# Expert slots of a mixture-of-experts stage: weight split first, output copy one slot later, gathers released by the transposes

## The reference, cut to what matters

```python
def hier_moe(h, w_group, b_group, w_expert, b_expert, w1, w3, w2):
    ...                                   # 4 groups x 8 experts, top 1 group, top 2 experts, weights
    hid = silu(einsum('td,edf->tef', t, w1)) * einsum('td,edf->tef', t, w3)   # d = 1024, f = 128
    hid = hid * combine[:, :, None]
    y = einsum('tef,efd->td', hid, w2)
```

## Time and profile before

| what | value |
|---|---|
| median of 3 runs | 2931.61 us (2927.03 to 2933.74) |
| profiled execution, its own time | 2928.18 us |
| its span | 2926.4 us |
| PE busy in the span | 2581.6 us (88%) |
| DVE, ACT, POOL busy | 1817.2, 921.5, 1474.8 us |
| slots of layer 0, first to last output copy | 374.1 to 598.6 us |
| slots of layer 1, first to last output copy | 1165.8 to 1393.5 us |

### The profile page before, as it was taken

The page is one execution under the profiler, slowest core; times in us unless marked ns, Lnnn a source line. Parts: engine busy times, 40 slices in busy tenths (PEclk is TensorE's granted clock), DMA queues, the critical chain, the costliest instruction groups (busy, mean ns, idle before and its releaser), DMA issues.

```text
span 2926.4 us, 36370 instructions
## 1 busy us (share of the span) xinstructions
PE 2581.6 (88%) x12686; PEld 2013.5 (69%) x12686; DVE 1817.2 (62%) x2136; ACT 921.5 (31%) x1315; POOL 1474.8 (50%) x1258
## 2 busy tenths in 40 slices
PE   4888799959999997999598999999964569999998
PEld 3765677747777776777386478888853558888887
DVE  6768765656777766656647376662259962666414
ACT  2023266723444423666212322221122221322102
POOL 4720333335444451333463047667767726776775
PEclk8978799979999997999698799999977889999999
DMA  8846478842323223887322023332420003333222
GB/s 302 265 139 220 158 273 299 294 129 81 94 94 100 86 87 109 310 291 259 127 75 70 1 56 88 100 100 90 123 75 1 1 1 87 94 93 100 94 94 79
DMA packets 316240, 375.70 MB, mean 128 GB/s; under 512 B 51258, under 2 KB 258894, under 8 KB 316022
## 3 DMA queue, kind: packets, MB, share of 16 engines
q1 hardware_dynamic: 258832, 326.14, 34.1%
q10 hardware_dynamic: 34150, 26.77, 3.1%
q0 software_dynamic: 23168, 21.59, 2.2%
HBM read 392.11 MB, written 49.90 MB: 151 GB/s over the span
## 4 chain that ended last, share of the span: by engine, by line
PE 30%; POOL 22%; issue 22%; DVE 13%; DMA 10%; ACT 2%; SPq 0%; POOLq 0%; ACTq 0%; DVEq 0%
POOL WL L790 15%; POOL WH L786 5%; PE PAIR L501 5%; PE PAIR L502 4%; PE PAIR L503 4%; PE PAIR L1786 3%; DMA ADA_A<-in_ada_w 2%; PE BANK L2212 2%; PE BANK L501 2%; DVE ADA_SUM L606 2%; PE BANK L502 2%; PE BANK L503 2%; DMA XG<-htok_scratch,GATHER_I 2%; PE PAIR L1756 2%; DMA W2RAW<-in_moe_w 2%
## 5 line engine op out<-in xcount | busy, mean ns | idle before, releaser
L790 POOL TENSOR_TENSOR WL<-RAW,WH 128x512 fp32r<-128x512 f32 x584 | 814.9, 1425 | 12.2
L501 PE MATMUL PAIR<-HH,WH 128*128 128x512 f32 x1792 | 710.0, 396 | 40.4 <-POOL HL L1080 30.7
L502 PE MATMUL PAIR<-HL,WH 128*128 128x512 f32 x1792 | 700.6, 391 | 0.0
L503 PE MATMUL PAIR<-HH,WL 128*128 128x512 f32 x1792 | 700.1, 391 | 0.0
L785 POOL TENSOR_TENSOR TURN<-ONES 128x1 f32<-128x1 f32 x146 | 35.6, 244 | 932.3 <-PE PAIR L503 849.3
L501 PEld LDWEIGHTS PAIR<-HH,WH 128*128 128x128 f32 x1792 | 338.1, 189 | 124.7 <-issue 41.9
L503 PEld LDWEIGHTS PAIR<-HH,WL 128*128 128x128 f32 x1792 | 338.2, 189 | 71.2
L502 PEld LDWEIGHTS PAIR<-HL,WH 128*128 128x128 f32 x1792 | 338.5, 189 | 70.9 <-issue 2.4
L786 POOL TENSOR_SCALAR WH<-RAW 128x2048 fp32r<-128x2048 f32 x146 | 281.9, 1931 | 0.0
L1885 DVE TENSOR_TENSOR WL<-RAW,WH 128x2048 fp32r<-128x2048 f32 x78 | 181.9, 2334 | 58.7 <-ACT WH L1707 58.7
L1961 POOL DMA_INDIRECT y_scratch<-OG,SCATTER_I x78 | 80.2, 1028 | 225.7 <-ACT OG L1842 219.3
(11 more groups left out here) (507 smaller groups left out, 4652.5 us busy)
## 6 DMA issues: line engine op xcount, KB each, us to landing
RAW<-in_moe_w SPq DMA_DIRECT2D x156, 512.0 KB, 4.7
RAW<-in_ffn_w_up SPq DMA_DIRECT2D x88, 512.0 KB, 4.9
W2RAW<-in_moe_w SPq DMA_DIRECT2D x78, 512.0 KB, 7.3
ADA_B<-in_ada_w SPq DMA_DIRECT2D x30, 1024.0 KB, 5.4
RAW<-in_ssm_w_in SPq DMA_DIRECT2D x48, 512.0 KB, 4.9
ADA_A<-in_ada_w SPq DMA_DIRECT2D x18, 1024.0 KB, 7.7
RAW<-in_ffn_w_down SPq DMA_DIRECT2D x32, 512.0 KB, 4.0
RAW<-in_ev_w_in SPq DMA_DIRECT2D x20, 512.0 KB, 4.8
```

The source lines that it names most:

```text
L501: nc.tensor.matmul(o, wh, xh, start=start, stop=False)
L502: nc.tensor.matmul(o, wh, xl, start=False, stop=False)
L503: return nc.tensor.matmul(o, wl, xh, start=False, stop=stop)
L790: ins = pool.tensor_tensor(WL[:, s, c], RAW[:, s, c], WH[:, s, c].bitcast(F32), ALU.subtract)
```

## The change

ACT's step is now weights(s+1), output(s-2), rows(s+1), turned(s-1), hidden(s). The output copy lags one slot more, so ACT's loop starts with two steps written out (`lead=2`) and ends one later. DVE's step has weights(s+1) ahead of rows(s+1). POOL's gather(s) waits for the transposes of slot s - 2 (`w["rows"]`) in place of DVE's `GL`, and the scatter placed behind gather(s+2) is that of slot s - 3. PE and SP keep their order. The number of instructions of each engine's computation is unchanged.

```diff
-    def slot_loop(eng, first, step, per):
+    def slot_loop(eng, first, step, per, lead=1):
         first()
-        step(None, 0)
-        passes = (SLOTS - 2) // 2
+        for s in range(lead):
+            step(None, s)
+        passes = (SLOTS - 1 - lead) // 2
         with eng.loop(passes, per) as e:
-            for s in (1, 2):
+            for s in (lead, lead + 1):
                 step(e, s)
-        for s in range(2 * passes + 1, SLOTS + 1):
+        for s in range(lead + 2 * passes, SLOTS + lead):
             step(None, s)
...
         def step(e, s):                               # ACT
+            if stage(e, s, -1) and (s or e is not None):
+                weights(e, s + 1)
+            if stage(e, s, 2):
+                output(e, s - 2)
             if stage(e, s, -1):
                 rows(e, s + 1)
             if stage(e, s, 1):
                 turned(e, s - 1)
-            if stage(e, s, -1) and (s or e is not None):
-                weights(e, s + 1)
             if stage(e, s):
                 hidden(e, s)
-            if stage(e, s, 1):
-                output(e, s - 1)
-        slot_loop(act, first, step, {w["rows"]: 2, w["down"]: 2})
+        slot_loop(act, first, step, {w["rows"]: 2, w["down"]: 2}, lead=2)
...
             if stage(e, s, -1):                       # DVE
-                rows(e, s + 1)
                 if s or e is not None:
                     weights(e, s + 1)
+                rows(e, s + 1)
...
         def gather(s):                                # POOL
             if s >= 2:
-                p = rows_pair(layer, s - 2)
-                pool.e.wait_ge(evac[p % 2], p // 2 + 1)
+                pool.e.wait_ge(w["rows"], SLOTS * layer + s - 1)
...
         for s in range(SLOTS):
             if s + 2 < SLOTS:
                 gather(s + 2)
-            if s >= 2:
-                scatter(s - 2)
-        scatter(SLOTS - 2)
-        scatter(SLOTS - 1)
+            if s >= 3:
+                scatter(s - 3)
+        for s in range(SLOTS - 3, SLOTS):
+            scatter(s)
```

## The result

The changed kernel takes 2916.21 us in the median of 7 runs (2913.55 to 2922.37), the kernel before 2931.88 us (2927.03 to 2942.79). The ratio is 0.9942 with an interval of 0.9928 to 0.9956: 13 to 21 us faster, clear of noise. The forecast was 2904 us; the measured time lies in the stated range, but outside the forecast's own part of it (2893 to 2909 us), in the part that belonged to rival A. The two profiled executions differ by 9.1 us (2928.18 and 2919.03 us).

The account below looks back on a forecast made before the run. Bound: an ACT-DVE-PE ring of 5.83 us per slot plus late W2RAW loads. Slots of 5.98 and 6.06 us becoming 5.65 save 27.4 us: 2928.18 to 2900.8, plus 3.4 for the median, about 2904 us; range 2892 to 2923.

Parts of the forecast that it names:

- rival A: Slot stages: a new wait (late scatter holding OG, or DMA share 0.89) takes half the gain: 2915 us, chance 0.22.
- The ring: Slot stages: output copy, GH, HT, WH, WL, HID, PE's products chained, 11.65 us per two slots; cutting it gains 21.5 us.
- PE's bound: Slot stages: PE's own work in a slot where nothing is late, 5.54 us.
- W2RAW: Down product's w2 load: issued at T + 0.1, 2 us earlier, no longer late; worth 14.1 us at most.
- T: PE's start of the transposes, rows(s+1), from which times within a step are counted.
- POOL held by WL: POOL's gather: WL holds it until T + 3.9, where scatter starts; price 0 while landing stays under 8.8 us.
- rival A's OG ring: Slot stages: a scatter landing L after its start makes OG's reuse ask (2.35 + L)/2 per slot; 9.25 gives 5.80.
- RAW itself gains nothing: RAW load in slot stages: its ring, with 4.7 us landing, takes 9.6 us per two slots, under 11.08.
- theory 5: Follow-up hypothesis: gather's and scatter's rows just ahead delay the RAW load; reordering cuts RAW waits under 50 us from 79.
- what would remain: Slot stages: PE and DMA limits, too near to be met at once, leave a slot of 5.65 us against 5.54.
- B: ACT's step: WH at its head waits for RAW, the rest queues behind; 11 us slower, 2943 us, chance 0.07.
- C: Slot stages: no change; PE already 95% busy, the ring reappears as a DMA bound near 6.0 us; chance 0.06.

Follow-up runs that it names:

- e2: POOL's two edits alone, put into the kernel before; ACT and DVE in the old order: 2937.32 us, 1.0019 to the kernel before.
- e1: The full change with POOL's two edits undone, so the new order on ACT and DVE alone: 2915.75 us, 0.9943 to the kernel before.
- e6: The full change without the output copy's extra lag (ACT copies slot s - 1 last, POOL scatters s - 2): 2947.24 us, 1.0037 to the kernel before.
- e3: The full change with DVE in the old order, rows(s+1) ahead of weights(s+1): 2971.54 us, 1.0133 to the kernel before.
- e5: The full change with WL made in two halves, the first releasing the first RAW load: 2899.38 us, 0.9883 to the kernel before.
- e8: The full change with POOL's scatter of slot s - 2 as before, the gather queued behind it: 2912.18 us, 0.9924 to the kernel before.
- e4: The full change loading only an eighth of w2 per slot from slot 2 on, output not the reference's: 2906.08 us, 0.9910 to the kernel before.

## Why the prediction was right, and where its sum was off

The direction and its cause were right. That the time fell into the stated range is partly luck: the slot missed its own part of the range, 5.50 to 5.72 us, and the range held only because rival A, with another mechanism, had been given the place next to it.

- **The ring: right.** Over all slots, the distance between PE's starts of the transposes two slots apart was 11.65 us in the median before, the ring's own number, and 11.6 in e2. In the changed kernel it is 10.9 to 11.0 us. e2 keeps the ring and gains nothing, e1 has only the new order of ACT and DVE and gains all. e6 closes another ring, through the output copy, WL and GL, and is 11 us slower than before; e3 makes WL late, so that RAW's ring rules, and is 40 us slower. Undisturbed slots take 5.44 us, 0.1 less than the 5.54 that I took as PE's bound from one slot.
- **W2RAW: right.** It is issued at T + 0.34, and the wait for it, the longest piece of the chain before, is off the list in the changed kernel. What it was worth by itself isn't shown.
- **POOL held by WL: right in mechanism, and no price is seen.** The gathers' median went from 1.01 to 1.95 us, and the scatter of the slot shown starts at T + 4.3 (forecast 3.9). ACT waited for a scatter 3 times, 1.6 us in all. So rival A's OG ring is not where the gain went. That holding the gather until just behind the RAW issue adds to the wait for RAW is not ruled out. In the slot shown the gather's issue ends at 467.82, 0.89 us behind the end of WL at 466.93. With WL in halves (e5, second row) the longest issue is 2.04 us in place of 3.11:

```profile
L1954 POOL DMA_INDIRECT XG<-htok_scratch,GATHER_I x78: 988/1952/3112, 356.9 to 1361.5; - x78
```
```profile
L1957 POOL DMA_INDIRECT XG<-htok_scratch,GATHER_I x78: 984/1426/2042, 354.3 to 1340.1; - x78
```

- **"RAW itself gains nothing" with a landing of 4.7 us: the step that was mis-sized.** I took 4.7 us as the landing of the second load of a pair and found slack in a ring of 9.6 us per two slots. But that row is the median over first and second loads together, and the first lands sooner. For the two loads of the pair issued at 453.32 the trace of the kernel before has:

```profile
DMA to landing us min/median/max: 4.3/5.0/5.7
```

  Over both stages before, the first loads landed in 4.3 us and the second in 6.0 us (medians), so ACT could start 6.5 us behind the first issue, not 5.1. The ring was then (4.93 + 6.0)/2 = 5.47 us per slot, just under PE's bound, and any longer landing would show. In the changed kernel the later load lands 7.1 us behind the first issue in the median and 7.2 in the mean (from the landing events of the trace). The ring measured is 0.18 (WL's end to the issue) + 7.2 + 0.16 (mean, until WH starts) + 1.91 (WH) + 0.04 + 2.29 (WL) = 11.8 us per two slots, about 5.9 per slot, against slots of 5.83 and 5.84 us. In most slots WH starts within 0.2 us of the landing; before, it was 1.0 us in the median. So this ring is the new bound. Of the 2 us that it was taken too short, some 1.4 are the misread row and 0.6 the longer landing.

  Why the landing grew by 0.6 us stays open in part. With the order of e8 and e1 on POOL it is back at 6.4 us in the median. But e2 speaks against the plain form of theory 5. There POOL's edits alone took the gather from 2.5 us ahead of the RAW issue (kernel before) to 1.1 us behind it and the scatter from 1.3 to 2.4 us behind, and the landing grew from 6.5 to 7.1 us. The kernel before had both the gather ahead and the scatter behind, as the full change has, and landed in 6.5 us. So neither of the two places is the whole reason, and no run moved one of them alone. e4 and e5 show that the wait yields both to fewer bytes and to an earlier release.

  I had put 0.11 us per slot on what would remain; it measured 5.83 - 5.44 = 0.39 us. That is 0.28 x 74 = 21 us; PE's bound, 0.10 us lower than taken, gives 7 us of it back, and the rest, 14 us, is the distance from the forecast's 27 us to the stages' 13.7 us.
- **The rivals.** B had the place (ACT's head, waiting for RAW), and not the size: by its formula (4.93 + L)/2 a second load that lands 6.8 us behind its own issue (the mean) gives 5.86 us, the slot that was measured. Its threshold for a loss, 7.1 us, was not reached. A had the time, by another mechanism than the one written down; that its figure of 2915 us came within 2 us is luck. C's DMA bound near 6.0 us is refuted by the full change itself and by e5, whose slots take 5.64 and 5.57 us.
- **Against the median:** the runs give 15.7 us, the stages of the two profiles 13.7 us. The rest of the profiles differs by more than that either way (the slot stage of layer 0 began 5 us later in the second one), and what happens there was not looked into.

## What to carry to other kernels

When a stall goes, the load behind it inherits the bound: recompute each double buffer's ring (release, issue, landing, use). Take the landing of the last load that the user waits for, not the median over all loads, and lengthen it for the higher rate. A buffer that one instruction frees and two transfers fill should be freed in two pieces; here that gave 17 us where moving whole steps had given 16. And an edit that measures as zero next to another bound, as POOL's did, can be worth keeping once that bound is gone.

## What the runs showed of the hardware

An indirect DMA issued from POOL while DVE runs a subtraction of two SBUF operands (WL) is held until that instruction ends, and ends about 0.9 us behind it, but only if it comes after the subtraction by enough. Those that started up to 0.04 us behind WL's start took 1.0 us, as nearly all did before the change (450.82 against 450.79 in the earlier trace rows). Those that started 0.07 us or more behind it were held: 3.11 us at 0.07 us behind in the changed kernel, 3.04 us at 0.13 us behind before. No issue fell between 0.04 and 0.06 us. So in the full change the 78 gathers take 1.95 us in the median and 3.11 at most. Beside a subtraction with one operand in PSUM (GL) they take 1.0 us. No wait of PE or ACT names the hold as its cause, save the 1.6 us for scatters.

Two loads of 512 KB, issued 0.43 us apart on one queue, did not land 0.43 us apart: from its own issue the first took 4.3 us and the second 6.0 us in the median (kernel before).

Less expected: with the issue of the gather (at most 128 rows) begun 1.9 us ahead of that of 1 MB of weight loads and the scatter's 1.0 us behind it, ScalarE waited 71 us more over 78 slots than with the scatter 0.8 us ahead and the gather 1.0 us behind (79.1 against 7.6 us, full change against e8).
